# Seven pairs of second-layer conditioning units summed on GpSimd during the first MLP instead of four

## The reference, cut to what matters

```python
cond = jax.nn.silu(c)
for l in range(DEPTH):                      # DEPTH = 2
    mod = cond @ w_ada[l] + b_ada[l]        # [1024] @ [1024, 6144]
    sh1, sc1, g1, sh2, sc2, g2 = jnp.split(mod, 6, axis=-1)
    h = _rms_norm(x, norm1_gain[l]) * (1.0 + sc1) + sh1
    ...                                     # projection, four head groups: o
    x = x + g1 * (o @ w_out[l])
    h = _rms_norm(x, norm2_gain[l]) * (1.0 + sc2) + sh2
    x = x + g2 * _conv_glu_ffn(h, w_ffn_up[l], ffn_conv_w[l], ffn_conv_b[l], w_ffn_down[l])
```

## Time and profile before

| | |
|---|---|
| median of 3 runs | 766.56 us (766.08 to 768.04) |
| profiled execution | 767.26 us, of which the span from first to last instruction is 765.5 us |
| PE busy | 730.5 us (95%) |
| PEld busy | 688.8 us (90%) |
| DVE busy | 500.2 us (65%) |
| ACT busy | 395.6 us (52%) |
| POOL busy | 120.0 us (16%) |
| DMA | 158.37 MB, mean 207 GB/s |

### The profile page before, as it was taken

The page is one execution under the profiler, slowest core; times in us unless marked ns, Lnnn a source line. Parts: engine busy times, 40 slices in busy tenths (PEclk is TensorE's granted clock), DMA queues, the critical chain, the costliest instruction groups (busy, mean ns, idle before and its releaser), DMA issues.

```text
span 765.5 us, 15006 instructions
## 1 busy us (share of the span) xinstructions
PE 730.5 (95%) x6249; PEld 688.8 (90%) x6249; DVE 500.2 (65%) x879; ACT 395.6 (52%) x633; POOL 120.0 (16%) x91
## 2 busy tenths in 40 slices
PE   5868999999999999999999999999999999999996
PEld 4558788899899999999998888899989999999995
DVE  2335577754679797978667456775558666666674
ACT  3237745554474656556544764554447544544532
POOL 2001100402205354463200010030400000000001
PEclk9689999999999999999999989999999999999998
DMA  9997997827458777686934867192836555545601
GB/s 290 341 257 174 343 290 247 264 67 244 143 200 284 238 231 263 217 273 215 351 114 137 267 195 254 57 291 68 287 107 205 197 169 178 205 168 177 204 6 56
DMA packets 139543, 158.37 MB, mean 207 GB/s; under 512 B 4931, under 2 KB 133076, under 8 KB 139476
## 3 DMA queue, kind: packets, MB, share of 16 engines
q1 hardware_dynamic: 139476, 157.41, 64.3%
HBM read 155.76 MB, written 1.64 MB: 206 GB/s over the span
## 4 chain that ended last, share of the span: by engine, by line
PE 82%; DVE 5%; ACT 4%; issue 2%; POOL 1%; DVEq 0%; POOLq 0%; ACTq 0%
PE bank L863 23%; PE bank L864 22%; PE bank L865 22%; PE bank L877 4%; DVE w_lo L1506 2%; PE bank L1178 2%; ACT w_hi L1269 1%; PE bank L1193 1%; PE bank L1192 1%; PE bank L917 1%; PE bank L1074 1%; PE bank L1191 1%; ACT work L1421 1%; PE bank L893 1%; PE bank L1072 1%
## 5 line engine op out<-in xcount | busy, mean ns | idle before, releaser
L1506 DVE TENSOR_TENSOR w_lo<-raw,w_hi 128x2048 fp32r<-128x2048 f32 (+1 forms) x98 | 237.9, 2429 | 95.3 <-ACT w_hi L1269 95.3
L863 PE MATMUL bank<-act_hi,w_hi 128*128 128x256 f32 (+1 forms) x1008 | 290.4, 288 | 4.5 <-DVE w_lo L1506 2.0
L864 PE MATMUL bank<-act_lo,w_hi 128*128 128x256 f32 (+1 forms) x1008 | 286.4, 284 | 0.0
L865 PE MATMUL bank<-act_hi,w_lo 128*128 128x256 f32 (+1 forms) x1008 | 286.4, 284 | 0.0
L1269 ACT ACTIVATE w_hi<-raw 128x2048 fp32r<-128x2048 f32 (+1 forms) x98 | 184.7, 1888 | 142.1 <-PE bank L865 141.3
L863 PEld LDWEIGHTS bank<-act_hi,w_hi 128*128 128x128 f32 (+1 forms) x1008 | 193.7, 192 | 14.0 <-issue 11.8
L864 PEld LDWEIGHTS bank<-act_lo,w_hi 128*128 128x128 f32 (+1 forms) x1008 | 193.9, 192 | 0.1
L865 PEld LDWEIGHTS bank<-act_hi,w_lo 128*128 128x128 f32 (+1 forms) x1008 | 193.8, 192 | 0.0
L863 PE MATMUL bank<-mlp_hi,w_hi 128*128 128x256 f32 x384 | 109.1, 284 | 2.4 <-DVE mlp_lo L1802 2.4
L864 PE MATMUL bank<-mlp_lo,w_hi 128*128 128x256 f32 x384 | 108.6, 283 | 0.0
L865 PE MATMUL bank<-mlp_hi,w_lo 128*128 128x256 f32 x384 | 108.6, 283 | 0.0
(11 more groups left out here) (186 smaller groups left out, 866.1 us busy)
## 6 DMA issues: line engine op xcount, KB each, us to landing
direct<-in_w_ada SPq DMA_DIRECT2D x48, 1024.0 KB, 9.2
raw<-in_w_ffn_up SPq DMA_DIRECT2D x44, 1024.0 KB, 5.1
raw<-in_w_in SPq DMA_DIRECT2D x22, 1024.0 KB, 6.5
raw<-in_w_ffn_down SPq DMA_DIRECT2D x22, 1024.0 KB, 4.9
raw<-in_w_out SPq DMA_DIRECT2D x8, 1024.0 KB, 5.3
bias<-toeplitz SPq DMA_DIRECT2D x4, 384.0 KB, 9.7
heads_out<-in_x SPq DMA_DIRECT2D x1, 1024.0 KB, 5.3
out<-heads_out SPq DMA_DIRECT2D x2, 512.0 KB, 3.1
```

The costliest lines, as they stand in the source:

```text
L863: pe.matmul(dst, lh, rh, start=first, stop=False, skip_group_check=check)
L864: pe.matmul(dst, lh, rl, start=False, stop=False, skip_group_check=check)
L865: return pe.matmul(dst, ll, rh, start=False, stop=last, skip_group_check=check)
L1506: nc.vector.tensor_tensor(w_lo[n % RAW][:, s], raw[n % RAW][:, s], w_hi[n % RAW][:, s].bitcast(F32), ALU.subtract).then_inc(lo_done, 1)
```

## The change

It moves three pairs of the second layer from TensorE (attention of the second layer) to GpSimd (MLP of the first). GpSimd sums a pair in each of the steps 1 to 7, units 0 to 13, instead of in steps 2, 4, 6 and 8, units 0 to 7. The norm between the layers gets pairs 14 and 16 instead of 8 and 10. In the second attention pair 18 alone is left; it stands at the first place that the schedule has for a pair, unit 6, and the other three places stay empty. LAG is not changed.

```diff
-PAIR_FROM = [SETUP_ADA, NA // 2]
 PAIR_TO = NA - 4
-
-
-GAP_PAIRS = {1: [(0, PAIR_TO), (0, PAIR_TO + 2)], 2: [(1, SETUP_ADA), (1, SETUP_ADA + 2)],
+PAIR_FROM = [SETUP_ADA, PAIR_TO - 2]
+
+
+GAP_PAIRS = {1: [(0, PAIR_TO), (0, PAIR_TO + 2)], 2: [(1, PAIR_TO - 6), (1, PAIR_TO - 4)],
              3: [(1, PAIR_TO), (1, PAIR_TO + 2)]}
 GAP_BANKS = {1: (5, 6), 2: (3, 2), 3: (5, 6)}
 GAP_BANK = {p: b for n in GAP_PAIRS for p, b in zip(GAP_PAIRS[n], GAP_BANKS[n])}
-MLP_STEPS = [(2, 4, 6, 8), ()]
+MLP_STEPS = [tuple(range(1, 8)), ()]
 LAG = 2
...
     def pair():
-        s.append(late[0])
+        if late:
+            s.append(late[0])
 
     def pair_turn():
-        s.append(("pair_turn",) + late.pop(0)[1:])
+        if late:
+            s.append(("pair_turn",) + late.pop(0)[1:])
```

## The result

The changed kernel takes 785.56 us (median of 5 runs, 781.89 to 786.15) against 766.56 us of the kernel before (766.08 to 768.04): a ratio of the runs of 1.0215, 95% interval 1.0182 to 1.0247 (the two medians divided give 1.0248). It is slower, as forecast, but by 19.0 us where 9.5 were forecast, and outside the range of 768 to 783. The profiled execution took 785.68 us with a span of 784.0, which is 18.5 more than the span before.

What follows compares the result with a forecast made beforehand. TensorE, busy 95% of the span, was taken to bound the kernel. Columns +3.8, first stall +3.7, later lock +6.9 and attention -4.9 sum to +9.5 us on 766.56, giving 776.1 us; range 768 to 783.

Steps and rivals of the forecast that it cites:

- The sign: Whole kernel: the change makes it slower, above 768.9 us, with chance 0.80.
- the columns: First MLP: seven sets of columns cost TensorE 0.95 us each where three did before, +3.8 us.
- the attention: Second attention: three pairs taken off TensorE, two worth 2.3 us each and the one at unit 9 0.3: -4.9 us.
- Part 2, the first stall: First MLP, before down(0): GpSimd's multiply for pair 1 and VectorE take turns, so TensorE stalls 3.7 us.
- rival C: TensorE's stalls drop its clock to the 1.2 GHz level, one to three falls at 3 us: 779 to 785; chance 0.12.
- Part 3, the lock in later steps: First MLP, steps 2 to 8: GpSimd and VectorE alternate, 20.3 us a step against TensorE's 18.2; stalls of 6.9 us.
- SyncE's queue: First MLP: value loads wait behind pair loads, 11 to 13 us behind TensorE's point; charged 0.
- Rival D: First MLP: value loads landing 2 us later than counted become the bound, +4 to 8 us: 780 to 784; chance 0.08.
- The sum: Whole kernel: first MLP +14.4 us and second attention -4.9 give +9.5, a median of 776.1 us.
- The signs: First MLP: VectorE busy 16 to 18 us, TensorE idle 3.7 before down(0), columns 20.3 apart mid-run, value loads some 10 later.
- The last loads: End of first MLP: the last four conditioning loads wait for pair 7, done about T9, and cost 0.

Runs made afterwards that it cites:

- run 2: Changed kernel with GpSimd's multiply and adds in the first MLP replaced by memsets that read nothing, conditioning sums left out: 769.13 us, ratio 1.0006.
- run 8: Changed kernel with pair loads behind value and down loads, steps 2 to 8, norm's pair loads behind last down load, attention's pair at unit 9: 773.38 us.
- run 10: The kernel of run 8 with the next layer's first two projection loads ahead of the norm's pair loads: 763.35 us, ratio 0.9936.
- after: The changed kernel itself, against the kernel before: 785.56 us, ratio 1.0215.
- run 1: Changed kernel with each step's conditioning pair loads behind its value and down loads instead of ahead of them: 769.94 us, ratio 1.0004.
- run 7: Changed kernel with the second attention's one pair at unit 9 instead of unit 6: 781.48 us, ratio 1.0151.
- run 5: Kernel before, still with four pairs, the first in step 1 instead of step 2 (steps 1, 4, 6, 8): 773.72 us, ratio 1.0075.
- run 4: Changed kernel with the seven pairs in steps 2 to 8 instead of 1 to 7: 786.55 us, ratio 1.0225.
- run 6: Changed kernel with loads of pairs 2 to 7 behind their steps' value and down loads, only pair 1's ahead: 776.67 us, ratio 1.0114.
- run 3: The kernel of run 2 with 4.8 us of further memsets ahead of each pair's last sum: 769.55 us, ratio 1.0020.

## Why the prediction was wrong, point by point

**The sign, the columns and the attention** were right. Columns: 3.8 forecast, 3.5 measured (run 2), and with one set in the last wait 2.9 forecast for run 8 and 2.9 measured in run 10. Attention: -4.9 forecast and measured, in after and in run 1; run 7 confirms that the place decides what a pair is worth.

**Part 2, the first stall**, was right in place, releaser and size (3.7 forecast, 3.27 measured, 4.12 in run 5), and not in its working. The multiply came 1.6 us later than laid out, relative to TensorE's step, since the pair landed 9.5 us after its issue in place of 7.8; the product was not held, the low part of down 0 was instead. What the sum had at nothing is the clock: 1.7 us behind this stall, 5.1 in the MLP. The prediction had it only as rival C, with 0.12, though its own show a fall behind a wait. By the Trainium skill ("TensorE: Matmul & The Clock Gate", section "Why this matters for your kernels") gaps of microseconds between bursts of matmuls bring the lower clock; here all eight idle times of 3.3 to 7.6 us did (after, runs 4 to 8), and of those of 1 to 2 us some did (1.06 in after, 0.98 in run 6, 1.75 in run 7) and some did not (1.74 in after, 1.06 in run 4, 0.98 in run 1). A spell costs 1.7 us and not 3, so one would have given 778 and three 781, by the forecast's sum.

**Part 3, the lock in later steps**, had the right cycle and the wrong payer. Forecast: 20.3 us a step for a whole pair; measured 21.0 in run 1. But the step that I took from it, "from there the lock is never free", so TensorE loses what exceeds 18.2, does not follow. In run 1 the excess fell on GpSimd, which is wanted only two steps later (LAG = 2) and drifted by 17 us before the columns waited for it. With the loads on time it cost 1.5 us, not 6.9.

**SyncE's queue is the step that failed.** I had the value loads 11 to 13 us late, which is what after shows (11 us), and then wrote "I charge 0, since the lock already made TensorE late by as much". That let one term pay for the other, when both draw on the same slack. Late landings alone cost 3.0 us (run 3), stretched low parts alone 1.5 (run 1), and both in the same steps 9.1, two spells of lower clock in it. Of that the loads of pairs 2 to 7 ahead are 7.6 (after against run 6). Rival D had the mechanism ("late value loads become the bound"), at 4 to 8 us beside the lock and a chance of 0.08. It holds, but the term beside it was the one to take away.

**The sum.** For idle time of TensorE the forecast was 3.7 + 6.9 = 10.6 us, and after has 10.15 more than before. That looks like a hit and is none: by the runs the lock alone accounts for 1.5 of the 6.9, and the rest comes from the queue that was charged 0; two errors of opposite sign hid each other. So the step that failed in the mechanism is the 0 for SyncE's queue, and the one that failed in size is the 0 for the clock: the miss of the MLP, 19.6 against 14.4, is about its 5.1 us. The other 3.7 us of the profiled execution lie ahead of the MLP, in code that is unchanged; they are in no case of mine, and no run settles them. Without them this execution would be at 782, but 1 to 2 us of them come back in every kernel with the seven pairs.

**The signs.** TensorE did idle before down(0), the low parts were long, and value loads went out about 10 us late, as the list of signs had it; from the first to the fifth set of columns GpSimd was busy 72.6 of 76.2 us, VectorE only 58.9, which is 14 of 18 and not 16 to 18. The sets were not 20.3 us apart in the middle: in after they are 18.2, 18.7, 19.5, 19.8, 25.1 and 18.2 us apart, so the loss sits in few steps and not in each. The clock's falls differ by more than one, and by its own list that makes the prediction wrong.

**The last loads.** "The last four conditioning loads wait for pair 7 ...: 0" was right for after and by little: run 4 shows what a step later costs.

## What to carry to other kernels

Where one engine's wait holds a queue of loads, follow what stands behind it in that queue, step by step, to who needs it: in runs 4, 8 and 10 the same wait of the pair loads cost 7.6, 5.4 and 0 us by what came after it. An engine that works slower than the steps come costs little until its own lag is used up (1.5 us in run 1), so compare the excess times the number of steps with the lag. And when two delays draw on the same slack, neither may be charged at nothing because of the other: test each alone and then both.

## What the runs showed of the hardware beside that

- Writing alone doesn't hold VectorE up: beside GpSimd's memsets every low part takes 2.29 us, beside its multiply or adds up to 5.72 (run 3 against run 1 and after). Which engine begins first counts: in after a low part that began at 284.90 took 2.29 us, and the multiply behind it, at 285.01, took 5.67 instead of 3.62.
- Spells of TensorE's lower clock in the MLP lasted 3.4 us (1.7 us of work lost) behind most of the stalls that had one, 6.8 behind the one ahead of down(0) in run 7, which in after had 3.4, 10.2 with the 7.59 us of run 4 and 13.7 with the 5.39 us of run 8, both begun within the wait. The same stall of 1.06 us brought one in after and in run 7 and none in run 4.
- A load of 1 MB that went out behind two pair loads landed 9.37 us after its issue, when 7.8 was the figure of the earlier trace rows for a pair.
